# One channel block of a 31-tap depthwise convolution on TensorE through diagonal weights, seven on VectorE, none on GpSimd

## The reference, cut to what matters

```python
# h: (1, 256, 1024); three projections of 1024 columns each
a, b, g = split(h @ cv_w_in, 3)
u = a * sigmoid(b)                       # the gated linear unit
y[t, c] = cv_db[c] + sum(cv_dw[tap, c] * u[t + tap - 15, c] for tap in range(31))   # zeros outside
y = silu(layernorm(y) * cv_ln_g + cv_ln_b) * silu(g)
x = x + gate * (y @ cv_w_out)
```

## Time and profile before

| | |
|---|---|
| median of 3 runs | 1271.81 us (1266.48 to 1275.34) |
| the profiled execution | 1267.39 us |
| its span | 1265.4 us |
| TensorE's mean granted clock | 0.786 |
| TensorE, busy | 889.2 us (70%) |
| VectorE, busy | 822.7 us (65%) |
| ScalarE, busy | 258.6 us (20%) |
| GpSimd, busy | 360.9 us (29%) |

### The profile page before, as it was taken

The page is one execution under the profiler, slowest core; times in us unless marked ns, Lnnn a source line. Parts: engine busy times, 40 slices in busy tenths (PEclk is TensorE's granted clock), DMA queues, the critical chain, the costliest instruction groups (busy, mean ns, idle before and its releaser), DMA issues.

```text
span 1265.4 us, 17275 instructions
## 1 busy us (share of the span) xinstructions
PE 889.2 (70%) x6732; PEld 672.5 (53%) x6732; DVE 822.7 (65%) x2039; ACT 258.6 (20%) x515; POOL 360.9 (29%) x344
## 2 busy tenths in 40 slices
PE   7799998877797885875344534534443699469998
PEld 7799696875585573753121211211111488358887
DVE  2454465768889767755697777777665499961411
ACT  2411101125222323120021011110100343231200
POOL 0000011043344333423444444444443064400000
PEclk9899998988898896977555655555555699779999
DMA  9846599499999999999999999999999133113240
GB/s 371 335 172 257 188 410 388 144 423 420 408 405 421 410 422 421 424 418 421 420 420 420 420 421 419 414 420 420 412 421 388 70 134 133 66 67 107 106 153 34
DMA packets 51408, 402.48 MB, mean 318 GB/s; under 512 B 5632, under 2 KB 7936, under 8 KB 9088
## 3 DMA queue, kind: packets, MB, share of 16 engines
q0 software_dynamic: 40320, 293.62, 56.4%
q1 hardware_dynamic: 10144, 105.62, 21.1%
q10 hardware_dynamic: 864, 2.16, 0.5%
HBM read 400.32 MB, written 1.05 MB: 317 GB/s over the span
## 4 chain that ended last, share of the span: by engine, by line
DMA 19%; PE 15%; DVE 13%; issue 2%; POOL 1%; ACT 1%; DVEq 0%; ACTq 0%
DMA wring<-uv_dram,arena 19%; PE ps L814 10%; DVE arena L1764 7%; PE ps L542 2%; POOL wring L406 1%; DVE wring L1388 1%; PE ps L529 1%; PE ps L434 1%; DVE arena L1388 1%; DVE arena L1404 1%; PE ps L856 1%; DVE arena L1352 0%; DVE arena L1767 0%; PE ps L509 0%; DVE arena L1748 0%
## 5 line engine op out<-in xcount | busy, mean ns | idle before, releaser
L406 POOL DMA_INDIRECT arena<-uv_dram,arena x192 | 226.2, 1178 | 356.2 <-PE ps L542 282.6
L542 PE MATMUL ps<-arena 128*32 128x256 f32 x1536 | 159.1, 554 | 225.8 <-DVE arena L1404 225.8
L1388 DVE CUSTOM_DVE_ANT_0 arena<-arena 128x1024 f32<-128x1024 f32 x192 | 232.3, 1225 | 97.4 <-DMA arena<-uv_dram,arena 94.0
L542 PEld LDWEIGHTS ps<-arena 128*32 128x32 f32 x1536 | 52.2, 142 | 315.7 <-DVE arena L1404 268.7
L814 PE MATMUL ps<-xn,wring 128*128 128x256 f32 x640 | 145.4, 391 | 17.5 <-DVE arena L1748 9.9
L814 PEld LDWEIGHTS ps<-xn,wring 128*128 128x128 f32 x640 | 125.5, 197 | 37.3 <-issue 18.2
L455 PE MATMUL ps<-xn,wring 128*128 128x128 f32 x1024 | 127.6, 286 | 4.8 <-DMA wring<-units_dram 3.3
L455 PEld LDWEIGHTS ps<-xn,wring 128*128 128x128 f32 x1024 | 123.9, 202 | 12.2 <-issue 6.1
L933 ACT ACTIVATE gel<-dots 128x2 f32<-128x2 f32 x128 | 26.0, 203 | 464.0 <-DVE dots L1388 443.4
L542 PE MATMUL ps<-wring,arena 128*32 128x256 f32 x512 | 53.1, 554 | 72.6 <-DVE arena L1404 72.6
L406 POOL DMA_INDIRECT wring<-uv_dram,arena x64 | 74.5, 1164 | 103.3 <-PE ps L542 93.3
(11 more groups left out here) (244 smaller groups left out, 1155.9 us busy)
## 6 DMA issues: line engine op xcount, KB each, us to landing
wring<-units_dram SPq DMA_DIRECT2D x48, 2048.0 KB, 10.5
arena<-mod_dram POOLq DMA_DIRECT2D x24, 1024.0 KB, 10.0
arena<-uv_dram,arena POOLq DMA_INDIRECT x192, 14.2
hA<-x_t_dram SPq DMA_DIRECT2D x2, 512.0 KB, 19.5
arena<-mem_t_dram SPq DMA_DIRECT2D x1, 1024.0 KB, 12.8
arena<-keys_dram ACTq DMA_DIRECT2D x2, 512.0 KB, 5.6
wring<-uv_dram,arena POOLq DMA_INDIRECT x64
wring<-grp_dram SPq DMA_DIRECT2D x1, 1024.0 KB, 4.9
```

The lines of the kernel that those rows point to most:

```text
L406: pool.indirect_dma_start(ring[b], None, uv_d, bass.IndirectOffsetOnAxis(ap=idx[:, n:n + 1], axis=0)).then_inc(sem(f"row_in{b}"), 16)
L542: mm = pe.matmul(acc_ps(q)[G * c:G * (c + 1), :], lhsT=diag[:, s % 2, j, :], rhs=ring[b][:, D + 256 * c:D + 256 * (c + 1)], start=(p == 0 ...
L1388: post(V.tensor_tensor_reduce(out=ring[b][:, 0:D], in0=ring[b][:, 0:D], in1=x_rep[q % 2], scale=1.0, scalar=0.0, op0=ALU.mult, op1=ALU.add ...
```

## The change

GpSimd's additions, ScalarE's products and their ring are gone. Block 0 is convolved on TensorE: ScalarE builds 31 diagonal matrices (the 128x128 identity times the column of weights of one tap) into memory that the first block's expert stage has left, between its sigmoids. TensorE multiplies each with the shifted `ypad[:, 0]` and sums all 31 in one half bank, after `cv_g0` and ahead of `cv_g1`. ScalarE copies the sum out with the bias added, ahead of the silu of `cv_g0`. VectorE convolves the other seven blocks, and the places of its `glu` steps among the taps are new.

```diff
-            for i, b in enumerate(CONV_POOL):
-                for tap in range(1, CV_TAPS):
-                    n = i * CV_TAPS + tap
-                    if tap > 1:
-                        need(pool, "conv_sum", n - i - 1)
-                    need(pool, "product", n + 1)
-                    post(pool.tensor_tensor(yc[:, b], products[(n - 1) % PRODUCTS] if tap == 1 else yc[:, b], products[n % PRODUCTS], ALU.add), "conv_sum")
...
             last_unit("cv_g0", xn)
+            need(pe, "tap_diag", CV_TAPS)
+            need(pe, "glu", 1)
+            for tap in range(CV_TAPS):
+                mm = pe.matmul(ps[:, 7, 0:S], lhsT=tap_diag[:, tap, :], rhs=ypad[:, 0, tap:tap + S], start=(tap == 0), stop=(tap == CV_TAPS - 1))
+            post(mm, "conv_sums")
...
             gate_sigmoid(1)
-            need(act, "ypads")
-            need(act, "glu", CONV_POOL[0] + 1)
-            for i in range(4):
-                tap_products(0, 8 * i, min(8 * i + 8, CV_TAPS))
-                gate_sigmoid(2 + i)
-            need(act, "glu", CONV_POOL[1] + 1)
-            for i in range(4):
-                tap_products(1, 8 * i, min(8 * i + 8, CV_TAPS))
-                if i < 2:
-                    gate_sigmoid(6 + i)
-                elif i == 2:
-                    gate_silu("cv_g0", 0)
+            for tap in range(CV_TAPS):
+                last = post(act.activation(tap_diag[:, tap], ident, ACT.Copy, scale=col("cv_dw", 8 * tap)), "tap_diag")
+                if tap in (3, 12, 21):
+                    gate_sigmoid(2 + tap // 9)
+            for k in range(5, KB):
+                gate_sigmoid(k)
+            act.wait_ge(sem("conv_sums"), 1)
+            go(act.activation(yc[:, 0], ps[:, 7, 0:S], ACT.Identity, bias=col("cv_db", 0)), "conv_pe")
+            gate_silu("cv_g0", 0)
...
             glu(0)
-            conv_taps(0, 0, 16)
             glu(1)
-            conv_taps(0, 16)
+            conv_taps(1, 0, 16)
             glu(2)
-            conv_taps(2)
+            conv_taps(1, 16)
             glu(3)
-            conv_taps(3, 0, 20)
+            conv_taps(2, 0, 16)
             glu(4)
+            conv_taps(2, 16)
             glu(5)
-            conv_taps(3, 20)
-            conv_taps(4, 0, 14)
+            conv_taps(3, 0, 16)
             glu(6)
-            conv_taps(4, 14)
+            conv_taps(3, 16)
             glu(7)
-            conv_taps(6)
-            conv_taps(7)
+            for b in range(4, KB):
+                conv_taps(b)
```

More of the change, by code:

```diff
@@ L141 @@
 EARLY = 2
-PRODUCTS = 8
-CONV_POOL = (1, 5)
-CONV_DVE = (0, 2, 3, 4, 6, 7)
 def build(nc, x_t, mem_t, cols_d, c_d, const_d, small_d, keys_d, units_d, grp_d, mod_d, uv_d, out_d, dbg=None):
@@ L267, in build @@
         odd_taps = area(2816, S)
-        products = [area(3072 + S * i, S) for i in range(PRODUCTS)]
+        tap_diag = area(M4, CV_TAPS * P).rearrange("p (a c) -> p a c", a=CV_TAPS)
         yc, gT, ycn = (blocks(area(5120 + 2048 * i, 2048), KB) for i in range(3))
@@ L407, in _ @@
                                         ).then_inc(sem(f"row_in{b}"), 16)
-            for i, b in enumerate(CONV_POOL):
-                for tap in range(1, CV_TAPS):
-                    n = i * CV_TAPS + tap
-                    if tap > 1:
-                        need(pool, "conv_sum", n - i - 1)
-                    need(pool, "product", n + 1)
-                    post(pool.tensor_tensor(yc[:, b], products[(n - 1) % PRODUCTS] if tap == 1 else yc[:, b], products[n % PRODUCTS], ALU.add), "conv_sum")
-                need(pool, "conv_sum", (i + 1) * (CV_TAPS - 1))
-                signal(pool, "conv_pool")
         @block.tensor
@@ L824, in _ @@
             last_unit("cv_g0", xn)
+            need(pe, "tap_diag", CV_TAPS)
[3 more added lines that the diff above has]
+            post(mm, "conv_sums")
             def mean_of(order):
                 for k in order:
-                    if k in CONV_POOL:
-                        need(pe, "conv_pool", CONV_POOL.index(k) + 1)
+                    if k:
+                        need(pe, "conv_dve", k)
                     else:
-                        need(pe, "conv_dve", CONV_DVE.index(k) + 1)
+                        need(pe, "conv_pe", 1)
                     mm = pe.matmul(tile_ps("mean")[:, 0:S], lhsT=ones, rhs=yc[:, k, :], start=(k == 0), stop=(k == KB - 1))
@@ L1191, in _ @@
             shifted(0)
[L1193 to L1206, removed]
             def gate_sigmoid(k):
@@ L1770, in _ @@
             go(V.memset(ypad[:, :, 0:15], 0.0))
-            go(V.memset(ypad[:, :, 15 + S:], 0.0), "ypads")
+            go(V.memset(ypad[:, :, 15 + S:], 0.0))
             glu(0)
-            conv_taps(0, 0, 16)
             glu(1)
-            conv_taps(0, 16)
+            conv_taps(1, 0, 16)
             glu(2)
-            conv_taps(2)
+            conv_taps(1, 16)
             glu(3)
-            conv_taps(3, 0, 20)
+            conv_taps(2, 0, 16)
             glu(4)
+            conv_taps(2, 16)
             glu(5)
-            conv_taps(3, 20)
-            conv_taps(4, 0, 14)
+            conv_taps(3, 0, 16)
             glu(6)
-            conv_taps(4, 14)
+            conv_taps(3, 16)
             glu(7)
-            conv_taps(6)
-            conv_taps(7)
+            for b in range(4, KB):
+                conv_taps(b)
             need(dve, "mean_sb")
```

## The result

| | before | changed |
|---|---|---|
| median of the first 4 runs each | 1272.53 us (1266.48 to 1275.34) | 1256.24 us (1254.82 to 1256.40) |
| ratio, 95% interval | | 0.9876 [0.9839, 0.9912] |
| the profiled execution, its time / its span | 1267.39 / 1265.4 us | 1256.39 / 1254.6 us |
| second comparison, on another occasion | 1266.89 us (11 runs) | 1259.58 us (6 runs), ratio 0.9943 [0.9920, 0.9966] |

The intervals of the two ratios don't overlap. The profiled executions differ by 11.0 us (0.87%), which lies between them; why medians of a few runs are a coarse measure here is shown with the experiments.

The account below looks back on a forecast made before the run. VectorE's work from the second glu to its last block was taken as the bound; -8.5 us there and +0.5 in the tail gave -8.0, so 1259.4 or 1263.8 us, forecast between them at 1261.5, range 1254 to 1268.

Parts of the forecast that it names:

- stretch, changed kernel: VectorE from the end of the second glu (1020.36 us) to its last block's end, forecast at 1112.5 us.
- 31 diagonals on ScalarE: Building the diagonals between sigmoids: at most 0.41 us each, 12.8 us in all, no sigmoid late, nothing on the path.
- TensorE's slack at the last sum: Second pair of cv_g1 ends near 1107.3 us, 5.2 us ahead of VectorE's last block.
- The bound and the slowdown: VectorE's 100.66 us bound the stage; 27.8 of them are slowdown, each GpSimd addition costing VectorE one wait.
- The glus' two clocks: VectorE's half blocks plus glu and TensorE's 6.89 us pairs run side by side, waiting some 0.1 us at times; 0.3 us added.
- TensorE's part costs nothing: Diagonal matmuls between cv_g0 and cv_g1, 62 instructions in 13.9 us, covered by VectorE's last block.
- the point of 0.34 us per instruction: Pitch of the diagonal matmul instructions from which TensorE's cover is gone and it decides the end.
- The tail: Behind VectorE's last block: 0.5 us more, for a last channel sum at the lower clock (1.22 instead of 0.70 us).
- TensorE as the bound: Rival: diagonals at 554 ns take 34.3 us, last channel sum 4.8 us later, 1272.2 or 1276.6 us; 5%.
- glus that throttle VectorE by 0.5 to 1 us each: Rival: six glus each wait that long, gain falls to 2 to 5 us, 1264.5 to 1267.5 us; 12%.
- The full-clock tail: Rival: diagonals keep TensorE's clock up; variance's sum gains 3.0, output projection 2.6 us; 1255.5 or 1253.4 us; 6%.
- That the slowdown isn't GpSimd's: Rival: VectorE's slow taps have another cause and stay, giving 1287 us; 2%.

Follow-up runs that it names:

- no_adds: Kernel before with only GpSimd's last addition of each of its two blocks, the other 58 left out: 1236.78 us against 1266.36 for before on that chip.
- after_gp_adds: Changed kernel plus 60 GpSimd additions of 128x256 on spare buffers that nothing reads: 1281.69 us.
- one_matmul: Changed kernel with one of the 31 diagonal matmuls (tap 15), the other 30 left out: 1256.80 us.
- matmuls_twice: Changed kernel with the 31 diagonal matmuls issued twice: 1259.03 us.
- adds_no_products: Kernel before without ScalarE's 62 products, GpSimd making its 60 additions on unscaled inputs: 1262.41 us.
- split_taps: Changed kernel with block 1 instead of 0 and nine taps of block 7 on TensorE, second cv_g1 pair behind the variance's sum: 1250.05 us, 0.9859 of before.

## Why the prediction was right, point by point

The places from the end of glu 1 on, in microseconds (each kernel's first profile):

| | forecast | measured |
|---|---|---|
| VectorE's undisturbed block | 12.61 | 12.62 (1099.26 to 1111.88); 12.65 from one block's start to the next (1086.61 to 1099.26) |
| stretch, changed kernel | 92.1 (1112.5 less 1020.36) | 92.35; 92.3 in the three other profiles with this order and no additions |
| slowdown by the additions | 27.8 | 26.9 (no_adds), 27.3 (after_gp_adds) |
| 31 diagonals on ScalarE | at most 12.8 | nine in 2.75, so 9.5 for all; no sigmoid late |
| 62 matmul instructions | 13.9 | 13.55 |
| TensorE's slack at the last sum | 5.2 | 5.05 |
| last channel sum | 1.22 | 1.15 |
| tail | +0.5 | -1.7 |
| sum | -8.0 | -10.8 (span) |

- **The bound and the slowdown.** Right, and shown from both sides: taking the additions from the kernel before and putting them into the changed one move the stretch by 27 us each. That each addition costs VectorE one wait held for additions in a row; no_adds shows two that cost it at most one (0.83 instead of 0.42 us) and waited themselves.
- **The glus' two clocks.** Right: VectorE is never idle for more than 0.15 us at the glus 2 to 7. The sum of VectorE's own work was 91.8 us, with 0.3 for the two clocks missing each other 92.1; measured are 92.35. That the 0.3 came so near is partly luck: of the 0.55 us above 91.8, about 0.3 lie at the six glus (3.67 us instead of 3.4), and the rest is the 0.04 us from a block's end to the next one's start, which a block of 12.61 us leaves out.
- **TensorE's part costs nothing.** Right (one_matmul). With the work doubled it came to decide, as the point of 0.34 us per instruction said.
- **The tail** is the term that was mis-sized, with the wrong sign. The 0.5 us at the last channel sum came (1.15 against 0.70), but the variance's sum took 5.27 instead of 6.58 and the output projection 29.55 instead of 30.40. The prediction took both over from the trace of before as fixed, and +0.45 - 1.31 - 0.85 are the -1.7 us. Both run for a part at the lower clock and go over to the full one on the way, and where this happens differs: over all kernels of this study that keep a gap of some 2.6 us ahead of it, the variance's sum took 5.1 to 6.6 us.
- **The number.** The convolution gave 8.3 us of the 8.5 forecast. That the sum reads -10.8 instead of -8.0 is the tail (2.2 us) and 0.8 us ahead of glu 1, where nothing was changed.
- **The chances.** The first comparison, 0.9876, is faster by over 1%, for which 0.23 stood; the second, 0.9943, lies within 1%, for which 0.71 stood. The traces say 0.9915 to 0.992. The forecast of 1261.5 us is 5.3 and 1.9 us above the two medians; set against the profiled execution alone it would have been 1259.4.
- **Rivals.** TensorE as the bound, and glus that throttle VectorE by 0.5 to 1 us each, are both excluded by the first profile. The full-clock tail came for a part (2.2 of 5.6 us), though not by the mechanism named, diagonals that keep TensorE busy: without 30 of the 31 the tail is 142.7 us as well (one_matmul). That mechanism is seen only with the work doubled, in matmuls_twice, where the variance's sum took 3.69 us. That the slowdown isn't GpSimd's is excluded by no_adds and after_gp_adds.

The prediction named the idle time that the new order puts between glu 0 and glu 1 (6.41 us measured) and priced it correctly (a block less counts only 6.4 us), but didn't see it as something the same edit could have kept.

**What stays open.** What moves the clock's rise within the tail is not settled. A part of the spread lies ahead of the convolution, and it is only located: over 13 profiles of all kernels here, VectorE's first step behind the experts' last sum starts between 997.0 and 1002.6 us, and no kernel changes what runs ahead of it. Within the tail the long run of projections took 57.0 us in two profiles and 55.49 in the others, which isn't explained either.

## What to carry to other kernels

Before work is given to GpSimd beside a busy VectorE, the price is to be read on VectorE: here 60 additions of 128x256 took 27 us from it, more than the work they saved. The sign in a trace is a known instruction form whose pitch doubles (0.40 to 0.83 or 0.88 us) in just the windows in which GpSimd is on, whatever ScalarE and DMA do. And when work is moved off the bounding engine, take the part that runs while that engine is busy, not the part that fills its wait: exchanging two blocks was worth 6.3 us, three quarters of what the change itself gave in the stretch (8.3 us). Where the time ahead of the edit varies by more than the gain, compare the stretch in the traces first and the medians second.

## What the runs showed of the hardware

- Beside GpSimd's chained additions VectorE gets through one tap for each addition: a tap every 0.83 us where additions are 0.81 us apart (adds_no_products), every 0.88 us where they are 0.86 apart (the kernel before). A glu, which reads one input from PSUM, stays at 0.42 us beside them (at 1033.09 us in the kernel before); the two `tensor_scalar` behind it do not (0.93 and 0.89 us instead of 0.41 and 0.35). A lone addition between taps took 5.63 and 9.65 us (no_adds).
- GpSimd that only writes SBUF leaves VectorE's two-input instructions at 0.40 us each, but a one-input `tensor_scalar` took 1.97 instead of 0.35 us beside a memset.
- The granted clock can fall in a TensorE gap of 2.6 us. In split_taps TensorE ran on to 1104.2 us, with one gap of 1.06 us ahead of the last channel sum, and the variance's sum, 2.59 us later, began at the lower level. In matmuls_twice, where TensorE had no gap from 1001.81 us to its last channel sum, a gap of 2.87 us left it at full clock (3.69 us for the variance's sum). The windows of split_taps (columns as in the earlier trace rows):

```profile
1104.00:1106.00 2.00, 0.19 (x1) 0.00 (x0) 1.23 (x3) 1.67 (x2) 0.00 (x0) 1.00 0.00 0
1106.00:1108.00 2.00, 1.22 (x3) 1.07 (x4) 1.26 (x3) 1.99 (x4) 0.00 (x0) 0.67 0.00 0
1108.00:1110.00 2.00, 2.00 (x6) 1.55 (x6) 0.00 (x0) 0.20 (x1) 0.00 (x0) 0.50 0.00 0
1110.00:1112.00 2.00, 2.00 (x11) 1.77 (x10) 0.00 (x0) 0.00 (x0) 0.00 (x0) 0.98 0.00 0
```

- An fp32 matmul of 128x128 weights and 256 columns is two instructions in the trace, 0.44 us in all at full clock, and it takes a moving operand at any start column at that price: 62 instructions on `ypad` from columns 0 to 30 in 13.55 us, 32 on aligned blocks in 7.07.
